# Attention's normalising products on GpSimd instead of VectorE

## The reference

```python
def _rmsnorm(x, g):
    y = xf * lax.rsqrt(jnp.mean(xf * xf, axis=-1, keepdims=True) + EPS)
    return (y * g)
...
    qkv = h @ w_qkv                                   # 256 x 3072
    q, k, v = jnp.split(qkv, 3, axis=-1)
    q = _rmsnorm(q.reshape(B, S, H, 2, d), q_norm)    # H = 8 heads, 2 halves, d = 64
    k = _rmsnorm(k.reshape(B, S, H, 2, d), k_norm)
...
    p = jax.nn.softmax(s + bias)                      # causal, ALiBi
    a = p[:, :, 0] - lam * p[:, :, 1]
    o = einsum(a, v)                                  # per head 2d = 128 wide
    o = _rmsnorm(o, subln_g) * (1.0 - lambda_init)
    return o.reshape(B, S, H * 2 * d) @ w_out
```

## Time and profile before

| | |
|---|---|
| median of 3 runs | 999.09 us (998.18 to 999.73) |
| profiled execution, its own time | 998.9 us |
| its span | 996.9 us |
| PE busy | 965.1 us, 97% of the span |
| DVE busy | 779.0 us, 78% |
| ACT busy | 479.0 us, 48% |
| POOL busy | 44.1 us, 4% |
| attention in this span | about 696 to 808 us |

### The profile page before, as it was taken

How to read it: one execution, slowest core, us unless ns; L and a number is a source line. 1 busy time by engine, 2 the same in 40 slices (tenths; PEclk the granted TensorE clock), 3 DMA queues, 4 the chain that set the end, 5 groups by cost and what they waited for, 6 DMA issues and landing times.

```text
span 996.9 us, 13078 instructions
## 1 busy us (share of the span) xinstructions
PE 965.1 (97%) x4504; PEld 797.6 (80%) x4504; DVE 779.0 (78%) x1463; ACT 479.0 (48%) x727; POOL 44.1 (4%) x64
## 2 busy tenths in 40 slices
PE   4999999999988999999999999999999899999998
PEld 3788888888977888888888888888877678888887
DVE  4897887776958787878788878786767689787873
ACT  5553544565233644435455435355767665353531
POOL 0100000010210200000000000000203000000000
PEclk9999999999989999999999999999999999999999
DMA  9966555573837457474656474645643135746431
GB/s 329 317 212 211 182 197 205 183 241 118 265 108 252 135 188 236 147 246 155 228 183 204 149 246 142 237 159 179 213 167 127 43 127 180 243 151 227 163 132 43
DMA packets 128445, 186.16 MB, mean 187 GB/s; under 512 B 5936, under 2 KB 104368, under 8 KB 128400
## 3 DMA queue, kind: packets, MB, share of 16 engines
q1 hardware_dynamic: 123744, 169.89, 50.1%
q0 software_dynamic: 4368, 14.96, 4.6%
q10 hardware_dynamic: 288, 0.72, 0.2%
HBM read 184.50 MB, written 1.05 MB: 186 GB/s over the span
## 4 chain that ended last, share of the span: by engine, by line
PE 87%; DVE 5%; DMA 3%; ACT 2%; issue 1%; POOL 1%; SPq 1%; DVEq 0%; ACTq 0%
PE pg L440 16%; PE pg L446 16%; PE pg L444 16%; PE acc L440 11%; PE acc L444 11%; PE acc L446 11%; PE acc L612 4%; DMA raw<-in_ffn_w_in 3%; DVE w_lo L1150 2%; PE pt L517 1%; POOL mix L406 1%; ACT w_hi L814 1%; SPq L324 1%; DVE mix L1425 1%; ACT mix L964 0%
## 5 line engine op out<-in xcount | busy, mean ns | idle before, releaser
L1150 DVE TENSOR_TENSOR w_lo<-raw,w_hi 128x1024 fp32r<-128x1024 f32 x320 | 374.2, 1221 | 29.2 <-ACT w_hi L814 27.9
L814 ACT CAST w_hi<-raw 128x1024 fp32r<-128x1024 f32 x320 | 315.8, 1046 | 23.5 <-DMA raw<-in_ffn_w_in 22.8
L440 PE MATMUL pg<-w_hi,a_hi 128*128 128x512 f32 x720 | 281.6, 391 | 0.0
L446 PE MATMUL pg<-w_hi,a_lo 128*128 128x512 f32 x720 | 280.5, 390 | 0.0
L444 PE MATMUL pg<-w_lo,a_hi 128*128 128x512 f32 x720 | 280.5, 390 | 0.0
L1239 DVE STREAM_TRANSPOSE mix<-hs 32x128 f32<-32x128 f32 x640 | 193.8, 303 | 9.6
L446 PEld LDWEIGHTS pg<-w_hi,a_lo 128*128 128x128 f32 x720 | 135.2, 188 | 28.2
L440 PEld LDWEIGHTS pg<-w_hi,a_hi 128*128 128x128 f32 x720 | 135.4, 188 | 27.9 <-issue 0.4
L444 PEld LDWEIGHTS pg<-w_lo,a_hi 128*128 128x128 f32 x720 | 135.3, 188 | 27.6
L1231 DVE SCALAR_TENSOR_TENSOR hs<-pg,rstd,hs 128x256 f32<-128x256 f32 x80 | 38.3, 483 | 99.4 <-ACT hs L859 99.4
L859 ACT ACTIVATE hs<-pg,rstd 128x256 f32<-128x256 f32 x80 | 37.9, 475 | 159.7 <-PE pg L446 159.7
(11 more groups left out here) (122 smaller groups left out, 619.8 us busy)
## 6 DMA issues: line engine op xcount, KB each, us to landing
raw<-in_ffn_w_in SPq DMA_DIRECT2D x176, 512.0 KB, 5.0
raw<-in_ffn_w_out SPq DMA_DIRECT2D x88, 512.0 KB, 5.7
raw<-in_attn_w_qkv SPq DMA_DIRECT2D x24, 512.0 KB, 4.7
diags<-in_conv_diags POOLq DMA_DIRECT2D x20, 512.0 KB, 4.7
raw<-in_conv_w_in SPq DMA_DIRECT2D x16, 512.0 KB, 5.4
raw<-in_conv_w_out SPq DMA_DIRECT2D x8, 512.0 KB, 4.2
raw<-in_attn_w_out SPq DMA_DIRECT2D x8, 512.0 KB, 3.8
gain<-in_ffn_norm POOLq DMA_DIRECT2D x3, 512.0 KB, 4.9
```

What stands on the lines that cost most here:

```text
L440: mm = pe.matmul(dst[j], stat_hi, m_hi, start=first, stop=False)
L446: mm = pe.matmul(dst[j], stat_lo, m_hi, start=False, stop=last)
L814: nc.scalar.copy(w_hi[n % RING][:, cols], raw[n % RAW][:, cols]).then_inc(hi_done, 1)
L1150: nc.vector.tensor_tensor(w_lo[n % RING][:, cols], raw[n % RAW][:, cols], w_hi[n % RING][:, cols].bitcast(F32), ALU.subtract).then_inc(lo_ ...
```

## The change

DVE no longer multiplies. POOL does it, directly behind its own power for the same m and t (or g and t), after it has waited for that power's completion. The twelve products keep their shapes, and keep raising `qn_done` and `on_done`.

```diff
@@ POOL, in the loop over POWERS
                 pool.wait_ge(mean_done, n + 1)
                 nc.gpsimd.tensor_tensor(dst, src, exponent[:, 0:src.shape[-1]], ALU.pow).then_inc(power_done, 1)
+                if kind in ("qk", "out"):
+
+                    pool.wait_ge(power_done, n + 1)
+                    heads = dst.shape[-1]
+                    row = xg[:, 0, t * BANK:(t + 1) * BANK] if kind == "qk" else o_sb[:, t, :]
+                    row = row.rearrange("p (g d) -> p g d", g=heads)
+                    factors = dst.rearrange("p (g a) -> p g a", a=1).to_broadcast([P, heads, BANK // heads])
+                    nc.gpsimd.tensor_tensor(row, row, factors, ALU.mult).then_inc(qn_done if kind == "qk" else on_done, 1)
@@ DVE, attn
-                def norm(scaled, t, n, power, done):
-
-                    power_ready(*power)
-                    g = BANK // n
-                    factors = grr[:, t, 0:g].rearrange("p (g a) -> p g a", a=1).to_broadcast([P, g, n])
-                    nc.vector.tensor_tensor(groups(scaled, t, n), groups(scaled, t, n), factors, ALU.mult).then_inc(done, 1)
-
...
-                    for t in range(TT):
-                        norm(halves(0), t, DH, ("qk", m, t), qn_done)
-
...
                 norm_out(0, 0)
                 norm_out(0, 1)
-                for t in range(TT):
-                    norm(o_sb, t, P, ("out", 0, t), on_done)
                 step(10)
...
                 norm_out(1, 0)
-                norm(o_sb, 0, P, ("out", 1, 0), on_done)
                 norm_out(1, 1)
                 rest_o(1, 0)
-                norm(o_sb, 1, P, ("out", 1, 1), on_done)
                 tick(u + 13)
```

## The result

The changed kernel takes 1010.22 us, median of 4 runs (1006.57 to 1013.25). The kernel before, run beside it, took 999.21 (998.18 to 999.73). The ratio is 1.0108 [1.0086 to 1.013]: 11.0 us slower, where +9.3 and 1008.4 us were forecast. The profiled execution took 1009.9 us, its span is 1008.1, 11.2 longer than before. Its page answers to the earlier trace rows with

The account below looks back on a forecast made before the run. PE, busy 965.1 of 996.9 us, was taken as the bound, its waits paid in full. Delays of 1.3 + 2.0 + 3.4 + 1.8 + 0.8 = 9.3 us on the 999.09 median gave 1008.4 us, range 1003.5 to 1013.5.

Parts of the forecast that it names:

- P: Time of one POOL product of 128x512, taken as 1.4 us, with a range of 0.56 to 1.7.
- The second power now stands behind the first product.: POOL's queue, q and k: power, product, power, product makes t = 1 ready 3.5 + 2P after the first power began.
- the 0.1 taken: Assumed wait in us between each POOL power and its product; nothing to 0.2 was said to move the sum under 1.
- five terms: PE's lateness: m = 0 1.3, m = 1 2.0, m = 2 and 3 3.4, output 1.8 and 0.8 us; sum 9.3.
- Rival 1, the port: POOL's products and DVE's subtractions hold each other up at m = 0 to 2: 4.8 us more, 1013.2 us; 28%.
- A first call of the routine would explain the row as well.: Alternative reading of the span's first POOL power, which took 1.56 us against 0.70 for another of the same size.
- m = 0 and m = 1 add up: First two q and k passages: the delays of PE, 1.3 and 2.0 us, add.
- m = 2 gives back 0.3, and m = 3 repeats the delay: 1.9 late at m = 2, less the 0.3 wait before `values(4)`; 3.4 late in all by m = 3.
- the further half us: At m = 2, `biased(7)` only 1.1 us late behind `scores(7)` at 1.6, since DVE finishes `combined(6)` earlier.
- Output, 1.8 and 0.8: The two output passages: `values(8)` 1.8 us late at g = 0, PE 0.8 late at g = 1.
- Nothing between the places: Between the listed passages no further lateness, predicted as 0 from `values(8)` to g = 1.
- After attention nothing comes back: Behind attention PE is busy throughout and gives nothing back; the last FFN stays as long as before.

Follow-up runs that it names:

- Experiment 6: Changed kernel with only the t = 1 products of q and k on POOL, t = 0 and the output on DVE: 1001.52 us, ratio 1.0025.
- Experiment 3: Changed kernel with DVE holding back its subtractions until both POOL products of q or k are done: 1007.52 us, ratio 1.0087.
- experiment 1: Changed kernel with each of POOL's twelve products replaced by a memset of the same 128x512 row: 1002.71 us, ratio 1.0028.
- Experiment 9: Kernel before, with one GpSimd power added at its start on a buffer nobody reads: 999.12 us, one run.
- Experiment 8: Changed kernel with the second transposes of m = 0 and 1 moved later in PE's queue: 1009.02 us, ratio 1.0093.
- experiment 7: Kernel before, with `biased(6)` moved into DVE's wait for POOL at m = 2: 998.93 us, ratio 0.9998.
- experiment 5: Changed kernel with only the output's four products on POOL, the eight of q and k back on DVE: 1002.46 us, ratio 1.0033.
- experiments 4: Changed kernel with only the eight products of q and k on POOL, the output's four back on DVE: 1006.98 us, ratio 1.0084.

## Why the prediction came out right

The number was right by 1.8 us and the time lay in the range. The mechanism forecast is there, and it is the larger part. But of the sum one term was too large, one that the forecast had left to a rival was missing, and one had not been seen. They nearly cancel, and that the number came so close is luck: with the measured P the forecast's own sum is 5.3 us, not 9.3.

- **"The second power now stands behind the first product."** Right, and the main cause. Experiment 6, which takes the product out from between the powers of q and k, brings attention from +8.1 to +1.2, the port's hold on the second power included. Experiment 3 takes the port away and leaves q and k 5.0 us late of 7.5. The gaps between power and product at m = 0 are 0.07 and 0.09 us, close to the 0.1 taken. That a gap of nothing or 0.2 would move the sum by under 1 us was slightly off: the sum holds eleven such gaps, so it is 1.1.
- **The size of P, 1.4 us.** Too large: 1.04. The slope was right in kind (a product costs more per column than a memset) but twice the memset's, not three times. By the prediction's own five terms P = 1.04 gives 0.6, 1.3, 2.0, 1.1 and 0.4, about 5.3 us, not 9.3. The Trainium skill (GPSIMD Engine Reference, section 3.1), from which 1.12 was estimated, was the nearer one.
- **Rival 1, the port, held at 28%.** It is real. In POOL's rows it adds 1.3 us at m = 0, 1.3 at m = 1 and 0.7 at m = 2 (powers and products over 1.64 and 1.04), 3.3 in all against the 4.8 that the rival priced. Experiment 3 takes it away, and attention is 2.9 shorter. With it m = 0 and m = 1 come to 1.9 and 2.6, where the trace has 1.8 and 2.6. At m = 2 the pair started late, behind `combined`, which the first product held. So only the second product met the pair (0.56), and the power `combined` (0.18). The rival's total, 1013.2, was too high because it was laid on P = 1.4 and on 1.6 at each place. The Trainium skill (SBUF — State Buffer, "Who interferes with whom") has the second of the two block until the first is through, and only where GpSimd reads. The traces agree where a read comes second or a product first: 2.61 against 1.64 for a power, 3.21 against 2.36 for a pair, and nothing for a memset. They don't where a power of 8 columns is already running: it reads SBUF too, but a pair begun inside it kept its 2.36 (experiment 1). There the measurement decides.
- **"A first call of the routine would explain the row as well."** This was the step that kept the port out of the forecast. Experiment 9 shows that it was wrong. With P = 1.04 and the port's 3.3 the sum would have been about 8.6, of the 9.6 that arose outside the low clock.
- **m = 0 and m = 1 add up.** Right: 1.8 and 2.6. But PE's wait is not the only way in which lateness is handed on. Experiment 8 shows another, once PE's wait at m = 0 is gone: through ACT's wait for the transpose, its rounding, and the next unit's weights.
- **m = 2 gives back 0.3, and m = 3 repeats the delay.** Right in the main. `values(4)` has no wait, and experiment 7 shows this give-back by itself. But the further half us, `biased(7)` coming sooner because DVE is done with `combined(6)` earlier, did not come: `scores(7)` and `biased(7)` are both 1.6 late behind m = 1, where 1.6 and 1.1 were said, and DVE had idled 3.48 us for PE. m = 2 and 3 together cost 3.1, said 3.4. P = 1.04 and the port's 0.7 give 2.7.
- **Output, 1.8 and 0.8.** The trace has 1.7 and 0.4. The 1.7 agrees by luck: P = 1.04 gives 1.1, and 0.5 came from PE's slower transpose of 784.22 (1.12 instead of 0.66) and 0.2 from the second power of g = 0 (1.19 instead of 1.01, asked for while `combined` ran). The four products meet no pair of subtractions (experiment 5).
- **Nothing between the places.** Not quite: 0.9 us arose between `values(8)` and g = 1, where PE ran at half clock for most of 783 to 794. No experiment isolates this, but the traces put a price on it. From the power of g = 0 to that of g = 1, kernels with the output on DVE took 23.83 us at a mean granted clock of 1.00 (experiment 9), 24.18 and 24.16 at 0.93 (before, experiment 7), and 24.80 and 24.90 at 0.86 (experiments 4 and 6). So 0.9 for a fall from 0.93 to 0.81 is of the size to expect. What makes the clock fall is not shown. More lateness alone is not it: the clock was 0.86 in experiment 6, with hardly any delay in front, and 0.87 in experiments 3, 5 and 8. It may also be why this kernel spreads over 6.7 us from run to run: its fastest run has the highest mean clock over the span (0.991) and its slowest the lowest (0.987).
- **After attention nothing comes back.** Right: 176.8 us in both.

What stays open: how the last us or so divides. Attention was read from one profile of each kernel, 0.4 us at m = 2 and 3 has no term, and the 0.9 put down to the clock was read from the trace and not tried.

## What to carry to other kernels

Before work goes to an engine that has time, read what stands behind it in that engine's queue: here an idle engine at 4% made the whole kernel 1.1% slower, mainly because a 1.04 us product was put in front of a 1.64 us power that the path waits for. If the engine is GpSimd, look as well at what VectorE runs with two SBUF inputs at that moment, since a product held a subtraction here, and a subtraction held a product or a power, to its end. And an odd duration in the old trace (1.56 where 0.70 is usual) is worth one small experiment before it is explained away.

## What was not expected of the hardware

- A power that reads 8 columns is held for a whole subtraction, 0.97 us, when it is asked for inside one. A power that is already running held nothing: the pair in experiment 1 begins at 708.04 inside one that began at 707.08, and takes its 2.36. In the changed kernel the pair of 757.34 begins inside the power of 757.09, and takes 2.35.
- GpSimd gets in between two subtractions that stand back to back in VectorE's queue: the product of 707.29 runs after the first of the pair, not after both.
- Not only instructions with two SBUF inputs are held. In the changed kernel one of DVE's scalings at g = 1 (L1399, one input of 128x4), begun at 808.22 inside the product of 807.64, took 0.48 us instead of 0.17 and ended with the product. Experiment 5 has the same. The others of its shape kept their 0.17. No experiment looks at this by itself.
- PE's granted clock fell to 0.58 over 787 to 795, behind 7 us in which PE was idle for 3.1. With 2.3 idle in the same place before, it was 0.79 and soon over. Experiment 9, the same program from there on, idled the same 2.3 and kept a clock of 1.00 in both stretches. So the idling doesn't settle by itself whether the clock falls.
